# Input projection: 20 of 28 column blocks by seven quarter products, three selection tiles counted on ScalarE

## The chip, the cores and the metric

One core of one Trainium2 chip. The metric is the device time of one execution in microseconds (us), the median of several executions. TensorE is PE below, its weight loads PEld; VectorE is DVE, ScalarE is ACT, GpSimd is POOL, and SyncE (SP) only issues DMAs.

## The reference, cut to what matters

One inference step of a decoder trunk with two layers, all in float32. A prompt of 2048 tokens and 64 sample rows (8 sequences of 8 tokens) go through the same layers. Every layer starts with one combined input projection of the 1024 features of each token:

```python
h = jnp.einsum('btd,de->bte', x, w_in)
(cb, cc, ch, cg, sq, sk, sv, sg, dq, dk, dv, dg, iq, ik, iw) = split_in(h)
y_a = cb * conv(cc * ch) * silu(cg)              # 4 x 256 columns
y_b = stick_breaking(sq, sk, sv) * silu(sg)      # 4 x 384 columns
score = sum over 8 heads of relu(iq . ik) * iw   # the indexer
idx = top_k(score, 256)                          # per query
y_c = attend(rope(dq), rope(dk)[idx], dv[idx]) * silu(dg)
x = layer_norm(alpha * x + concat(y_a, y_b, y_c) @ w_out)
```

The keys and values, the last two rows of cc * ch and the new x are outputs too. The columns without the indexer's are 3584, which is 28 blocks of 128.

## The kernel before, in words

The program is written out by hand: each engine has one list of instructions per stage, with waits on semaphores, and a barrier of all engines stands between stages. A layer goes through seven of them: the indexer's projection and its scores for the prompt, the indexer for the samples (`sindex_*`), the input projection (`project_*` with `select_vector`), stick-breaking attention, sparse attention, the samples' attention, and the output projection. Memory is one tile, `arena`, that each stage cuts up anew; `banks` are the eight banks of PSUM, each 128 x 512 floats.

**PE in the projection** (`project_tensor`, lines 893 to 926). `xT` holds the tokens with the features on the partitions, in 8 chunks of 128 features. The 28 column blocks come in nine chunks of weights, `CHUNKS` (sk, c0, c1, dq, dkv, sv, sq, sg, dg); each is loaded while the one before it is used. Two kinds of units exist. A T unit (sk, dq, dkv, sv: 11 blocks) gives rows of 128 tokens: for each of 8 feature chunks a product with the tokens as weights and 384 or 256 columns moving (line 907). An F unit (c0, c1, sq, sg, dg: 17 blocks) gives 128 columns transposed: the weights stand and 512 tokens move (line 904). The 64 sample rows come once in each chunk (line 912). sk, dq and dk are needed in both forms, so their rows are transposed by PE as well (line 924, 112 transposes in a layer). A product in float32 is two instructions of PE in the profile; the counts in the profile are of those.

**ACT** (`project_scalar`) copies each unit out of its bank (lines 967, 969, 971), scales sq and dq, applies SiLU to the gates and copies the transposes (line 977). **POOL** (`project_gpsimd`) rotates dq and dk (the helper `rope`, lines 487 to 493) and computes the convolution with its gates (lines 1007 to 1024). **SP** (`project_sync`) stores everything and loads weights.

**DVE** (`select_vector`) takes no part in the projection: meanwhile it selects the 256 best scores of each query. The scores of 14 tiles of prompt queries (widths 384 to 2048) and of all sample queries (2056) lie in `arena`. In 32 passes it finds the threshold bit by bit: a pass counts for each tile how many scores reach the threshold (line 1057), writes the samples' comparison (line 1054), whose sum ACT takes (line 1044), and sets the next bit (lines 1073 and 1076). At the end, it marks the selected scores tile by tile, ties in order (lines 1082 to 1097). The next stage needs the marks, so the barrier waits for DVE too.

The output projection (lines 2281 on) already forms 2 x 2 blocks of its result from seven products in place of eight, with POOL and DVE making the sums. Its lines in the profile are used below.

## Time and profile before

| | us |
|---|---|
| median of 3 executions | 4497.47 |
| lowest, highest | 4490.78, 4499.33 |
| span of the profiled execution (first to last instruction) | 4494.1 |
| PE busy in it | 4186.5 (93%) |
| DVE busy | 3499.9 (78%) |
| ACT busy | 1748.9 (39%) |
| POOL busy | 1220.0 (27%) |

No time of the profiled execution other than its span is given; the span lies between the lowest and the highest of the three. The page divides the span into 40 slices and gives for each engine the busy share; shares over the whole span average stages with different limits, so the rows below are of single stages. A PE instruction's end is modelled, so durations of PE are best read as the distance between starts, or from the chain of waits.

### The profile page before, as it was taken

What the parts mean: (1) busy time and instruction counts of PE and PEld (TensorE: products, weight loads), DVE (VectorE), ACT (ScalarE), POOL (GpSimd) and SP (SyncE); (2) the same over time, 40 slices, a digit from 0 to 9 for tenths busy, and PEclk for the clock granted to TensorE, in tenths of its full rate; (3) what the DMA queues carried; (4) which work ended last, traced back from release to release, by engine and by line L of the source; (5) the groups of instructions that cost most, each with busy time, mean ns of one, the idle gap of its engine ahead of it and who ended that gap; (6) DMA issues with size and microseconds to landing.
All of it is one profiled execution on the core that took longest, in us unless ns stands there. A gap on an engine that the chain in (4) does not pass through costs nothing.

```text
span 4494.1 us, 81717 instructions
## 1 busy us (share of the span) xinstructions
PE 4186.5 (93%) x30510; PEld 2385.3 (53%) x30510; DVE 3499.9 (78%) x5677; ACT 1748.9 (39%) x2568; POOL 1220.0 (27%) x1531
## 2 busy tenths in 40 slices
PE   8988999999989999889989889999999999988898
PEld 5433545754466666454454335457544666764543
DVE  2686999999899865565637869999997998655656
ACT  3553211211067787340135632122111777873300
POOL 4220034500024242115442101355000333421154
PEclk9999999999999999889999999999999999998899
DMA  2102210211133102895311021112112330029942
...
DMA packets 328156, 397.11 MB, mean 88 GB/s; under 512 B 101079, under 2 KB 248626, under 8 KB 324434
## 3 DMA queue, kind: packets, MB, share of 16 engines
...
## 4 chain that ended last, share of the span: by engine, by line
PE 75%; DVE 7%; issue 6%; ACT 5%; DMA 4%; SPq 1%; ACTq 1%; POOL 1%; DVEq 0%; POOLq 0%
PE banks L904 21%; PE banks L907 14%; PE banks L2281 8%; PE banks L334 6%; PE banks L377 4%; PE banks L1549 3%; DVE arena L480 3%; PE banks L1519 3%; PE banks L1269 3%; PE banks L1231 2%; PE banks L1533 2%; PE banks L1253 2%; DVE arena L1376 1%; DMA arena<-in_cache_dsa_kv 1%; ACT arena L1579 1%
## 5 line engine op out<-in xcount | busy, mean ns | idle before, releaser
L1057 DVE TENSOR_SCALAR_CACHE_REDUCE arena<-arena 128x1920 uint8<-128x1920 f32 (+13 forms) x896 | 1259.0, 1474 | 0.0
L904 PE MATMUL banks<-arena 128*128 128x512 f32 x2176 | 937.4, 592 | 0.0
L904 PEld LDWEIGHTS banks<-arena 128*128 128x128 f32 x2176 | 410.6, 189 | 519.8 <-issue 519.5
L907 PE MATMUL banks<-arena 128*128 128x384 f32 (+1 forms) x2048 | 620.0, 459 | 2.4 <-POOLq L143 2.4
L1376 DVE TENSOR_TENSOR_SCAN arena<-arena 128x129 f32<-128x129 f32 (+3 forms) x480 | 512.3, 1127 | 22.1 <-ACT arena L1293 22.1
L480 DVE SCALAR_TENSOR_TENSOR arena<-arena 128x512 f32<-128x512 f32 (+3 forms) x532 | 404.4, 760 | 112.7 <-ACT arena L446 63.0
L907 PEld LDWEIGHTS banks<-arena 128*128 128x128 f32 x2048 | 380.8, 189 | 206.7 <-POOLq L143 2.6
L1614 DVE CUSTOM_DVE_ANT_0 arena<-banks,arena 128x512 f32<-128x512 f32 (+3 forms) x480 | 269.4, 607 | 159.5 <-PE banks L1519 158.8
L2281 PE MATMUL banks<-arena 128*128 128x512 f32 x896 | 387.2, 593 | 3.8 <-DVE arena L2407 1.7
L446 ACT ACTIVATE arena<-banks 128x1024 f32<-128x1024 f32 (+3 forms) x304 | 278.7, 920 | 236.6 <-PE banks L377 125.2
L377 PE MATMUL banks<-arena 64*128 64x512 f32 (+3 forms) x1216 | 309.5, 594 | 64.6 <-ACT arena L446 63.0
L334 PE MATMUL banks<-arena 128*128 128x292 f32 (+1 forms) x1088 | 312.9, 431 | 0.6 <-ACT arena L414 0.6
L971 ACT COPY arena<-banks 128x384 f32<-128x384 f32 (+2 forms) x144 | 70.5, 490 | 616.4 <-PE banks L907 361.3
L2281 PEld LDWEIGHTS banks<-arena 128*128 128x128 f32 x896 | 169.3, 190 | 218.9 <-issue 209.3
L1597 POOL TENSOR_SCALAR arena<-arena 128x128 f32<-128x128 f32 (+14 forms) x180 | 199.8, 1123 | 272.4 <-DVE arena L1625 272.4
L334 PEld LDWEIGHTS banks<-arena 128*128 128x128 f32 (+1 forms) x1088 | 191.7, 190 | 137.4 <-issue 89.4
L1307 ACT COPY arena<-banks 128x256 f32<-128x256 f32 (+3 forms) x240 | 216.1, 900 | 118.0 <-PE banks L1253 117.5
L1579 ACT COPY arena<-banks 128x1024 f32<-128x1024 f32 (+3 forms) x240 | 213.4, 889 | 121.1 <-PE banks L1533 120.4
L1567 ACT ACTIVATE arena<-arena 128x128 f32<-128x128 f32 (+15 forms) x192 | 231.1, 1204 | 4.0 <-DVE arena L1620 3.4
L1519 PE MATMUL banks<-arena 64*128 64x512 f32 (+3 forms) x960 | 211.2, 552 | 11.8 <-DVE arena L1614 9.8
L1549 PE MATMUL banks<-arena 128*64 128x128 f32 x3264 | 212.7, 277 | 8.3 <-DVE arena L1638 7.0
L1293 ACT ACTIVATE arena<-banks 128x256 f32<-128x256 f32 (+3 forms) x240 | 204.6, 896 | 36.0 <-PE banks L1231 21.7
...
## 6 DMA issues: line engine op xcount, KB each, us to landing
arena<-in_cache_sb_kv SPq DMA_DIRECT2D x256, 384.0 KB, 4.8
...
arena<-in_x_prompt SPq DMA_DIRECT2D x32, 512.0 KB, 3.9
...
arena<-xs SPq DMA_DIRECT2D x32, 512.0 KB, 4.0
arena<-in_cache_dsa_kv ACTq DMA_DIRECT2D x112, 128.0 KB, 5.3
...
```

Source lines behind the costliest of these rows:

```text
L334: m = nc.tensor.matmul(bank[v][r, 0:HALFW], xT[:, k, s * P:s * P + rows_of(s)], W1[:, k, v * HALFW:(v + 1) * HALFW], start=(k == 0), stop= ...
L377: k = nc.tensor.matmul(bank[4 + 2 * (i % 2) + e][:, 0:w], iqT[t % 2][a:a + HD, h, :], ikT[a:a + HD, c * FREE:c * FREE + w], start=True, st ...
L446: nc.scalar.activation(ir[b][:, :, 0:w], z[:, :, 0:w], ACT.Relu).then_inc(s_ir, 1)
L480: k = nc.vector.scalar_tensor_tensor(v, ir[b][:, h % 2, 0:w], wh, v, ALU.mult, ALU.add)
L904: m = nc.tensor.matmul(bank[i % 4][:, :], W2[c % 2][:, k, j * P:(j + 1) * P], xT[:, k, t * FREE:(t + 1) * FREE], start=(k == 0), stop=(k = ...
L907: m = nc.tensor.matmul(bank[i % 4][:, 0:WD[name]], xT[:, k, t * P:(t + 1) * P], W2[c % 2][:, k, 0:WD[name]], start=(k == 0), stop=(k == KC ...
L1057: nc.vector.tensor_scalar(dummy[j % 2][:, 0:v.shape[-1]], v, thr[:, t:t + 1], 0.0, ALU.is_ge, ALU.add, accum_out=history[:, k, t:t + 1]).t ...
L1376: nc.vector.tensor_tensor_scan(stay[n % 4][:, h, a:FREE + 1][:, ::-1], k, k, first, ALU.mult, ALU.min).then_inc(s_bs1, 1)
L1519: k = nc.tensor.matmul(bank[2 * (i % 2) + g][:, 0:w], dqT[q % 2][a:a + HD, c, t % 4 * P:(t % 4 + 1) * P], dkT[a:a + HD, x * FREE:x * FREE ...
L1549: k = nc.tensor.matmul(bank[6 + f % 2][a:a + HD, 0:P], dvn[:, kt, a:a + HD], weightsT(i)[:, o:o + P], start=(kt == 0), stop=(kt == t), ski ...
L1614: nc.vector.tensor_tensor_reduce(lg[e % 4][:, g, x * FREE:x * FREE + w], bank[2 * (i % 2) + g][:, 0:w], sc[:, SC_OFF[t] + x * FREE:SC_OFF[ ...
L2281: m = nc.tensor.matmul(bank[b], rows[:, k, :], cols[:, k, :], start=(first and k == 0), stop=(k == 3), skip_group_check=True)
```

## The change

**Products.** The 28 blocks are divided anew. 8 blocks (dq, dk; sv, dv) stay rows of 128 tokens, now in 34 units with 512 columns moving: first dq and dk ("qk"), then sv and dv ("vv"). The other 20 form ten pairs, `FBLOCKS`, and each pair is computed for two halves of 1024 tokens: 20 slots, m = 0 to 19. In a slot the result is 2 x 2 pieces (two blocks, two times 512 tokens), and the features are in two halves of 512. Seven products of 4 feature chunks each give what takes 8 such products in the old way. They stand in PE's list in the order 1, 6, 3 of the slot before, 5, 2, 7, 4; product 2 is added onto 1 in its bank, 7 onto 6, and 3 onto 5 after the bank has been read.

**Sums.** POOL makes, per half, four sums of tokens S1 to S4 (each 128 x 4 x 512) and, per slot, four sums of weights T1 to T4 (128 x 512 each). After the products, ACT copies banks to `fp1`, `fu2`, `fu3`; POOL adds `fp1` to `fu2` and `fu3` (`joined`); DVE adds a bank to one of them for three of the four pieces (`add_until`, 60 such adds in a layer, named "22", "21", "12" by token quarter and block). ACT applies SiLU to gated pieces in place. POOL does the convolution from the pieces in slots 1 to 4 and 11 to 14.

**Transposes and samples.** sk is now computed transposed and its rows come from PE's transposes; dq and dk as before: 112 transposes in a layer. The samples' rows come in 2 + 10 groups of 16 products, where nine were before.

**Selection.** From the second pass on DVE counts 11 tiles; the three longest (1792, 1920, 2048) are counted by ACT with `Sign(score - threshold)` and a sum, 93 counts in a layer. Their counts are compared with another bound (`cutv`). At the end DVE recounts these three twice to correct rounding. Where the adds stand among DVE's counts, and the counts among ACT's copies, is set by a table of due times in units of one product (4 chunks of 512 columns): `slot_at`, `unit_at`, `pass_at`, with PACE = 5.4 units for a pass.

**The rest.** `arena` grows by 4096 floats for each partition. Before the stage's barrier SP issues seven loads (six of 64 columns, one of 128) in place of one of 384. sq is no longer scaled when it is copied; the two sigmoids of the attention take the factor instead. Two buffers of the attention lie elsewhere. Weights of slot m + 1 are loaded after product 3 of slot m - 1.

```diff
--- before.py
+++ after.py
...
-            load_chunk(sp, l, 0)
...
+        PUNITS = [("qk", t) for t in ROWS_FIRST] + [("vv", t) for t in VALUES_FIRST]
...
+        FBLOCKS = (("cc0", "ch0"), ("cb0", "cg0"), ("cc1", "ch1"), ("cb1", "cg1"), ("sk0", "sk1"),
+                   ("sk2", "sq0"), ("sq1", "sq2"), ("sg0", "sg1"), ("sg2", "dg0"), ("dg1", "dg2"))
+        NFC = len(FBLOCKS)
+        NF2 = 2 * NFC
...
+        def load_row_weights(sp, l, v):
             src = w_in[l].rearrange("(c p) n -> p c n", p=P)
-            w, s = W2[c % 2], s_w2[c % 2]
-            if name in PERM:
+            if v == 0:
                 for h in range(HDSA):
                     d = (h % 3) * P + h // 3 * HD
-                    sp.dma_start(w[:, :, d:d + HD], src[:, :, COL[name] + h * HD:COL[name] + (h + 1) * HD]).then_inc(s, 16)
...
-                    a = col + P * (name == "c1")
-                    sp.dma_start(w[:, :, j * P:(j + 1) * P], src[:, :, a:a + P]).then_inc(s, 16)
+                    sp.dma_start(TW[0][:, :, d:d + HD], src[:, :, DQ + h * HD:DQ + (h + 1) * HD]).then_inc(s_tw[0], 16)
...
+        F_AT = 71.0
+        def slot_at(m, x):
+            extra = 0.7 * min(m, NFC - 1) + sum({5: 1.0, 6: 0.5}.get(e % NFC, 0) for e in range(m))
+            return F_AT + 7 * m + extra + x
...
+        def quarter(half, q, k):
+            a = (2 * half + q) * FREE
+            return xT[:, 4 * k:4 * k + 4, a:a + FREE]
...
+        def place(k, half):
+            if half:
+                return {"S3": quarter(0, 0, 0), "S2": quarter(0, 0, 1), "S4": quarter(0, 1, 1), "S1": quarter(1, 1, 0)}[k]
+            if k == "S1":
+                return quarter(0, 1, 0)
+            a = S_AT + (int(k[1]) - 2) * 4 * FREE
+            return arena[:, a:a + 4 * FREE].rearrange("p (c t) -> p c t", c=4)
...
+        def fbank(p, m):
+            return bank[{1: 4, 2: 4, 6: 5, 7: 5, 5: 6 + m % 2, 3: 6 + m % 2, 4: 0}[p]]
...
+            def onto_5(m):
+                fsummed(pe, l, m, "22")
+                fpool(pe, l, ("S4", m // NFC))
+                product(m, 3, wq(m, 1, 1), place("S4", m // NFC), first=False)
...
+            for m in range(NF2):
...
+                pe.wait_ge(s_w2[m % 2], at(s_w2[m % 2], 16 * (l * W2USES[m % 2] + loads)))
+                product(m, 1, wq(m, 0, 0), quarter(half, 0, 0))
+                if m:
+                    fevicted(pe, l, m - 1, "u3")
+                fpool(pe, l, ("S2", half))
+                fpool(pe, l, ("T2", m))
+                product(m, 6, fT[1], place("S2", half))
+                if m:
+                    onto_5(m - 1)
+                if m >= 2:
+                    fsummed(pe, l, m - 2, "12")
+                product(m, 5, fT[0], place("S1", half))
+                key_rows(m - 1, "11")
+                key_rows(m - 1, "22")
+                fevicted(pe, l, m, "p1")
+                product(m, 2, wq(m, 1, 0), quarter(half, 0, 1), first=False)
+                key_rows(m - 1, "21")
+                key_rows(m - 1, "12")
+                fevicted(pe, l, m, "u2")
+                fpool(pe, l, ("T3", m))
+                product(m, 7, wq(m, 0, 1), place("S3", half), first=False)
+                if m + 1 < NFC:
+                    sample(m + 1)
+                if m:
+                    fsummed(pe, l, m - 1, "21")
+                else:
+                    pe.wait_ge(s_pe, at(s_pe, l * NPE + NPU))
+                fpool(pe, l, ("T4", m))
+                product(m, 4, fT[2], quarter(half, 1, 1))
+            onto_5(NF2 - 1)
...
+                count_until(slot_at(m, 1))
+                fproduct(act, l, m, 1)
+                if m:
+                    fpool(act, l, ("u3", m - 1))
+                nc.scalar.copy(fp1, fbank(1, m)).then_inc(s_pe, 1)
+                count_until(slot_at(m, 2))
+                fproduct(act, l, m, 6)
+                if m:
+                    gate_piece(m - 1, "12", 10.3)
+                    fsummed(act, l, m - 1, "12")
+                nc.scalar.copy(fu2, fbank(6, m)).then_inc(s_pe, 1)
+                copy_key_rows(m - 1, "11")
+                copy_key_rows(m - 1, "22")
+                count_until(slot_at(m, 5))
+                fproduct(act, l, m, 2)
+                slot_free(act, l, m, "11")
...
+            def summed(name):
+                half = name[1]
+                a11, a12, a21 = quarter(half, 0, 0), quarter(half, 0, 1), quarter(half, 1, 0)
+                a22 = quarter(half, 1, 1)
+                out = place(name[0], half)
+                if name[0] == "S3":
+                    nc.gpsimd.tensor_tensor(out, a11, a21, ALU.subtract).then_inc(s_pp, 1)
+                elif name[0] == "S1":
+                    fpool(pool, l, ("S3", half))
+                    nc.gpsimd.tensor_tensor(out, a21, a22, ALU.add).then_inc(s_pp, 1)
+                elif name[0] == "S2":
+                    fpool(pool, l, ("S1", half))
+                    nc.gpsimd.tensor_tensor(out, place("S1", half), a11, ALU.subtract).then_inc(s_pp, 1)
...
+            def first_weight_sums(m):
...
+                if m:
+                    fproduct(pool, l, m - 1, 5)
+                nc.gpsimd.tensor_tensor(fT[0], wq(m, 0, 1), wq(m, 0, 0), ALU.subtract).then_inc(s_pp, 1)
...
+                nc.gpsimd.tensor_tensor(fT[1], wq(m, 1, 1), fT[0], ALU.subtract).then_inc(s_pp, 1)
...
+            def third_weight_sum(m):
...
+                nc.gpsimd.tensor_tensor(wq(m, 0, 1), wq(m, 1, 1), wq(m, 0, 1), ALU.subtract).then_inc(s_pp, 1)
...
+            def fourth_weight_sum(m):
...
+                nc.gpsimd.tensor_tensor(fT[2], wq(m, 1, 0), fT[1], ALU.subtract).then_inc(s_pp, 1)
...
+            def joined(m, name, out):
+                fevicted(pool, l, m, name)
+                nc.gpsimd.tensor_tensor(out, out, fp1, ALU.add).then_inc(s_pp, 1)
...
+        SIGNED = [NT - 1, NT - 2, NT - 3]
+        PASS = [NT, NT - 2, NT - 1] + [t for t in SELTILES if t < NT - 2]
+        PASS_V = [NT] + [t for t in SELTILES if t < NT - 3][::-1]
+        NCOUNT = len(PASS) + NBIT * len(PASS_V)
...
+        PACE, FIRST_PASS = 5.4, 7.4
...
+        def pass_at(k):
+            return 0.6 if k == 0 else FIRST_PASS + PACE * (k - 1)
...
+        def count_scalar(act, l, n):
+            k, j = scalar_count(n)
+            if j == 0:
+                act.wait_ge(s_cnt, at(s_cnt, counted_before(l, k) + 1))
+                nc.scalar.activation(compared[:, 0:NKEY], compared[:, 0:NKEY], ACT.Copy, accum_out=history[:, k, NT:NT + 1]).then_inc(s_sum, 1)
+            else:
+                t = SIGNED[j - 1]
+                v = scores(t)
+                act.wait_ge(s_bit, at(s_bit, l * NSTEP + 10 + 3 * (k - 1)))
+                act.wait_ge(s_sum, at(s_sum, l * NSUMS + n))
+                nc.scalar.activation(compared[:, 0:v.shape[-1]], v, ACT.Sign, bias=thr[:, t:t + 1],
+                                     accum_out=history[:, k, t:t + 1]).then_inc(s_sum, 1)
...
+            return {"22": slot_at(m, 6.9), "21": slot_at(m, 7.15), "12": slot_at(m + 1, 3.1)}[q]
...
+            def add_until(x):
+                while added[0] < NFSUM and vector_sum_at(added[0]) < x:
+                    m, q = FSUMS[added[0]]
+                    product, u, name = {"22": (5, fu3, "u3"), "21": (4, fu3, "u3"), "12": (3, fu2, "u2")}[q]
+                    slot_free(dve, l, m, q)
+                    fproduct(dve, l, m, product)
+                    fpool(dve, l, (name, m))
+                    nc.vector.tensor_tensor(hb[fslot(m, q)], fbank(product, m), u, ALU.add).then_inc(s_fsum, 1)
+                    added[0] += 1
...
-                for j, t in enumerate(PASS):
+                tiles = PASS_V if k else PASS
+                x, per = pass_at(k), PACE / sum(scores(t).shape[-1] for t in PASS_V)
+                for j, t in enumerate(tiles):
                     v = scores(t)
+                    add_until(x)
+                    x += per * v.shape[-1]
                     if t == NT:
-                        dve.wait_ge(s_sum, at(s_sum, l * NPASS + k))
+                        if k:
+                            dve.wait_ge(s_sum, at(s_sum, l * NSUMS + 1 + 4 * (k - 1)))
...
+                nc.vector.tensor_tensor(below, history[:, k + 1, :], cutv, ALU.is_lt).then_inc(s_bit, 1)
+                step(11 + 3 * k)
+                nc.vector.tensor_scalar(flip, below, float(1 << b), None, ALU.mult).then_inc(s_bit, 1)
...
+            x = pass_at(NPASS)
+            for j, t in enumerate(SIGNED):
+                v = scores(t)
+                add_until(x + 0.7 * j)
+                if j == 2:
+                    step(NTHR + 3)
+                nc.vector.tensor_scalar(dummy[j % 2][:, 0:v.shape[-1]], v, thr[:, t:t + 1], 0.0, ALU.is_gt, ALU.add,
+                                        accum_out=fix[:, t - NT + 3:t - NT + 4]).then_inc(s_bit, 1)
...
```

The lists of the three engines, as built:

PE, first layer. Before, the chunks sv and sq, behind the last transpose of the units before them (L907 rows of tokens, L904 blocks transposed, L912 samples; x16 are 8 feature chunks twice):

```order
L924 MATMUL banks<-ident,arena 128x128
L907 MATMUL banks<-arena 128x384 x120
L912 MATMUL banks<-arena 64x192 x16
L904 MATMUL banks<-arena 128x512 x96
L912 MATMUL banks<-arena 64x192 x16
```

The change, slots 4 and 5 (L1135 the quarter products, four to each; L1145 samples; L1155 transposes of sk):

```order
L1145 MATMUL banks<-arena 64x128 x16
L1135 MATMUL banks<-arena 128x512 x28
L1145 MATMUL banks<-arena 64x128 x16
L1135 MATMUL banks<-arena 128x512 x20
L1155 MATMUL banks<-ident,arena 128x128 x8
L1135 MATMUL banks<-arena 128x512 x4
L1155 MATMUL banks<-ident,arena 128x128 x8
L1135 MATMUL banks<-arena 128x512 x4
L1145 MATMUL banks<-arena 64x128 x16
```

A slot is 28 products of 512 columns where 32 stood for the same two blocks and 1024 tokens; samples come after every slot of the first half.

DVE, first layer. Before, the start of a pass (L1054 samples, L1057 counts):

```order
L1054 TENSOR_SCALAR arena<-arena 128x2056
L1057 TENSOR_SCALAR arena<-arena 128x1920
L1057 TENSOR_SCALAR arena<-arena 128x2048
L1057 TENSOR_SCALAR arena<-arena 128x384
L1057 TENSOR_SCALAR arena<-arena 128x512
L1057 TENSOR_SCALAR arena<-arena 128x640
```

The change, the start of a pass that runs beside the slots (L1509 samples, L1513 counts, L1496 the adds):

```order
L1509 TENSOR_SCALAR arena<-arena 128x2056
L1496 TENSOR_TENSOR arena<-banks,arena 128x512
L1513 TENSOR_SCALAR arena<-arena 128x1664
L1513 TENSOR_SCALAR arena<-arena 128x1536
L1513 TENSOR_SCALAR arena<-arena 128x1408
L1513 TENSOR_SCALAR arena<-arena 128x1280
L1513 TENSOR_SCALAR arena<-arena 128x1152
L1513 TENSOR_SCALAR arena<-arena 128x1024
L1496 TENSOR_TENSOR arena<-banks,arena 128x512
L1513 TENSOR_SCALAR arena<-arena 128x896
L1496 TENSOR_TENSOR arena<-banks,arena 128x512
```

The three longest counts are gone from the pass, and two or three adds that wait for PE and POOL stand between its counts.

POOL, first layer, the change, the middle of slot 11 (L1330, L1334 weights' sums T1 and T2; L1372 to L1384 a convolution; L1354 `joined`; L1340 T3). Before, no row of L1330, L1334, L1340 or L1354 existed:

```order
L1330 TENSOR_TENSOR arena<-arena 128x512
L1334 TENSOR_TENSOR arena<-arena 128x512
L1367 COPY arena<-arena 128x2
L1372 TENSOR_TENSOR arena<-arena 128x512
L1375 COPY arena<-arena 128x2
L1377 TENSOR_SCALAR arena<-arena 128x512
L1378 TENSOR_SCALAR arena<-arena 128x512
L1380 TENSOR_TENSOR arena<-arena 128x512
L1382 TENSOR_SCALAR arena<-arena 128x512
L1384 TENSOR_TENSOR arena<-arena 128x512
L1354 TENSOR_TENSOR arena<-arena 128x512
L1340 TENSOR_TENSOR arena<-arena 128x4x128
```

The sum `u3` (L1354) that DVE and then PE's product 3 need stands behind a whole convolution in such a slot.

## Rows read from the trace of the kernel before

**Rows 1.** The page: span, and part 1, busy time of each engine

```profile
span 4494.1 us, 81717 instructions
PE 4186.5 (93%) x30510; PEld 2385.3 (53%) x30510; DVE 3499.9 (78%) x5677; ACT 1748.9 (39%) x2568; POOL 1220.0 (27%) x1531
```

**Rows 2.** Busy time by stretch: the projection of both layers (columns: first row)

```profile
core 0: us, PE busy (x) PEld busy (x) DVE busy (x) ACT busy (x) POOL busy (x), PEclk, DMA share, GB/s
422.70:1232.80 810.10, 810.09 (x2512) 428.50 (x2512) 786.86 (x1057) 150.69 (x262) 162.38 (x280) 1.00 0.18 54
2655.30:3465.40 810.10, 810.08 (x2512) 428.47 (x2512) 786.87 (x1057) 150.62 (x262) 162.38 (x280) 1.00 0.18 54
```

**Rows 3.** Chain of waits, projection of layer 1: start, us, what

```profile
438.79 5.16 PE banks L907 x16
...
623.67 3.61 PE banks L912 x32
...
835.52 6.91 PE banks L907 x32
...
976.56 82.67 PE banks L904 x192
```

**Rows 4.** Timeline of PE: samples, and the stage's end

```profile
888.81 1.97 PE L912 MATMUL banks<-arena 128*64 128x128 f32 x32
...
1229.99 2.82 PE L912 MATMUL banks<-arena 128*64 128x192 f32 x32
1236.37 3.35 PE L1231 MATMUL banks<-arena 64*128 64x128 f32 x12 [3.56 <-SPq L143]
```

**Rows 5.** Timeline of DVE: two passes' starts, start and end of the marking

```profile
423.41 1.29 DVE L1054 TENSOR_SCALAR arena<-arena 128x2056 uint8<-128x2056 f32 x1
...
444.75 1.29 DVE L1054 TENSOR_SCALAR arena<-arena 128x2056 uint8<-128x2056 f32 x1
...
1110.69 0.72 DVE L1082 SCALAR_TENSOR_TENSOR arena<-arena 128x544 f32<-128x544 f32 x1
...
1214.18 2.36 DVE L1097 SCALAR_TENSOR_TENSOR arena<-arena 128x2056 f32<-128x2056 f32 x1
```

**Rows 6.** Groups by line and shape, 400 to 1260 us: busy, mean ns | idle before

```profile
L1057 DVE TENSOR_SCALAR_CACHE_REDUCE arena<-arena 128x2048 uint8<-128x2048 f32 x32 | 74.9, 2340 | 0.0
...
L1044 ACT ACTIVATE arena<-arena 128x2056 uint8<-128x2056 uint8 x32 | 61.4, 1919 | 0.0
...
L1054 DVE TENSOR_SCALAR arena<-arena 128x2056 uint8<-128x2056 f32 x32 | 41.9, 1310 | 1.4 <-DVE arena L1076 0.3
...
L1057 DVE TENSOR_SCALAR_CACHE_REDUCE arena<-arena 128x384 uint8<-128x384 f32 x32 | 19.4, 607 | 0.0
...
L969 ACT ACTIVATE arena<-banks 128x512 f32<-128x512 f32 x32 | 19.1, 597 | 189.7 <-PE banks L904 189.7
...
L1017 POOL TENSOR_SCALAR arena<-arena 128x512 f32<-128x512 f32 x16 | 12.2, 760 | 1.5
...
L1007 POOL TENSOR_TENSOR arena<-arena 128x512 f32<-128x512 f32 x8 | 10.2, 1276 | 109.8 <-ACT arena L969 109.7
...
L1093 DVE TENSOR_TENSOR_SCAN arena<-arena 128x2056 uint16<-128x2056 bf16 x1 | 4.4, 4442 | 0.0
```

**Rows 7.** Groups by line, output projection of layer 1, 2030 to 2260 us

```profile
L2281 PE MATMUL banks<-arena 128*128 128x512 f32 x448 | 193.5, 593 | 2.1 <-POOLq L143 1.5 <-DVE arena L2407 0.7
...
L2407 DVE SCALAR_TENSOR_TENSOR arena<-arena,banks 128x512 f32<-128x512 f32 x32 | 21.2, 682 | 38.6 <-PE banks L2281 38.6
...
L2209 POOL TENSOR_TENSOR arena<-arena 128x512 f32<-128x512 f32 x8 | 12.8, 1596 | 14.2 <-DMA arena<-mixT 11.8 <-PE banks L2281 2.4
...
L2197 POOL TENSOR_TENSOR arena<-arena 128x2048 f32<-128x2048 f32 x1 | 4.5, 4517 | 5.5 <-DMA arena<-in_w_out 5.5
```

**Rows 8.** DMA issues (KB each, us to landing), 400 to 1240 us

```profile
arena<-in_w_in SPq DMA_DIRECT2D x8, 512.0 KB, 6.1
...
arena<-in_w_in SPq DMA_DIRECT2D x12, 256.0 KB, 4.9
```

**Rows 9.** Timelines before the stage: SP's weight load, PE's last wait

```profile
401.03 0.44 SPq L813 DMA_DIRECT2D arena<-in_w_in  x1
...
408.73 1.97 PE L597 MATMUL banks<-ident,arena 128*128 128x128 f32 x8 [5.27 <-DMA arena<-in_cache_dsa_kidx]
```

874 lines of the change are left out of this document (581 added, 293 removed).

## The prediction

> **What bounds the kernel now.** I read the busy times first, then the table by stretch, the chain of waits in the stage, the timelines at its two ends, and the groups of its instructions. The span is 4494.1 us, PE busy for 93% of it [rows 1]; such a share tells little by itself, since stages differ. The table by stretch tells more: the projection is 810.1 us in either layer, 1620.2 us or 36% of the span, PE is busy for all of it at a granted clock of 1.00 (2.4 GHz), and DVE for 786.9 us [rows 2]. So two engines are full at once. Which of them ends the stage is read at its end: DVE's last mark begins at 1214.18 and is over at 1216.5 us [rows 5], PE's last samples begin at 1229.99, and the next stage begins at 1236.37 [rows 4]. PE bounds it, with DVE 16 us behind. Taking work from PE alone would therefore give 16 us in a layer at most; the reader should see why the change has to touch both.
>
> **PE, what goes.** An instruction of 512 columns costs 82.67 / 192 = 0.4306 us, of 384 columns 5.16 / 16 = 0.3225, of 256 columns 6.91 / 32 = 0.2159 [rows 3]. Before, a layer has 1088 of the first (17 blocks x 4 x 8 x 2), 768 of the second (9 blocks as 3 chunks x 16 x 8 x 2), 256 of the third: 468.5 + 247.7 + 55.3 = 771.5 us. After, 8 blocks as 2 x 16 units of 16 instructions are 512, and 20 slots of 7 products of 8 instructions are 1120, all with 512 columns: 1632 x 0.4306 = 702.7 us. That is **68.8 us less** in a layer. The transposes are 112 both times: nothing. Samples: before, six groups of 192 columns at 2.8 us, two of 256 at 3.6, one of 128 at 1.9 to 2.0 [rows 3, 4], 26.0 us; after, ten of 128 at 1.97 and two of 256, 26.9 us: **0.9 us more**. PE's own work goes from 810 to 742 us, 67.9 us less.
>
> Whether PE can run products of 4 chunks without pauses is seen in the output projection, which does so already: 448 instructions with 2.1 us of idle time before them [rows 7].
>
> **DVE, is it still covered?** A pass takes 444.75 - 423.41 = 21.34 us [rows 5]. A count costs 2340 ns at 2048 and 607 at 384 columns [rows 6], a slope of 1.04 ns, and less the overlap with its neighbour about 0.14 us + 1.04 ns a column. The three counts that leave have 5760 columns: 6.4 us less; one more small step of some 0.2 us: 15.1 us a pass. A layer: first pass 22, 31 passes 468, marking 1216.5 - 1110.7 = 106 [rows 5], recounts of 5760 columns twice 13 with steps 14, 60 adds of a bank at 0.68 (the output projection's [rows 7]) with gaps 43: 653 us against PE's 742. DVE is covered with 89 us to spare. Its adds wait in its list for PE and POOL, and behind a waiting add stand counts, behind those the next threshold, and ACT's counts wait for that; but as long as DVE is early, such a wait only keeps it in step.
>
> **ACT.** 2056 elements take 1919 ns [rows 6], so three counts of 5760 elements take 5.4 us and some tenths of a us each for start and reading the sum, 6.2, beside the 2.1 us for the samples' sum: 8.3 us of a pass of 18.6 us by the table. Copies at 0.6 us, four to seven in a slot of 24 to 26 us, add little. Covered; a copy can be late by one count, 2.2 us, against 6.9 us from product 7's end to product 6 of the next slot, which needs the copy.
>
> **POOL.** A sum of two tensors of 512 takes 1276 ns, a scaling 760 [rows 6], a sum of 2048 takes 4517 [rows 7]. A plain slot has six sums, 8 us of 24. S1 to S4 in slot 9 are 18 us more: 26 us, done before product 6 of slot 10 needs S2. In slots 1, 3, 11 and 13 two convolutions of 6.3 us stand in between. There the chain is: product 3 of the slot before ends 10.3 us into the slot, DVE adds (11.5), a convolution (18), u2, T1, T2 (22), the second convolution (28.6), u3 (29.9), DVE's add (30.7 and up to one count more). PE wants it for product 3, at 24.1 + 6.9 = 31.0 us in the second half, 33 in the first, where samples stand before it. So 0 to 2 us of waiting: I take 1 us x 4 = **4 us** a layer. Below it lies nothing; above, if all these sums took the 1596 ns of the output projection's [rows 7], the chain would be 3 us longer and the wait up to 4 us in each: 16 us.
>
> The Trainium skill (GPSIMD Engine Reference, Specifications) says that POOL's ports are shared with DVE and contended when DVE runs a two-port mode or reads two SBUF inputs. By this rule the chain keeps the 1276 ns, since DVE's counts and adds here read one SBUF tensor each; were the contention there all the same, it would be the 16 us.
>
> **DVE's marking.** The due times leave no room for adds there. Marking and recounts are 120 us, 5 slots; in these 15 adds of 0.7 us stand, 10.5 us of lag at its end. An add may be 6.5 us late before product 3 waits, less part of a scan of up to 4.4 us [rows 6] before it. I take **3 us**; bounds 0 and 10.5.
>
> **The stage's ends.** SP's one load of weights at 401.03 becomes seven; PE then waits 5.27 us for the last keys, which come while that load runs [rows 9]. A load of 256 KB lands in 4.9 us, of 512 KB in 6.1 [rows 8]. Queued in part before the keys, they delay the stage by **2 us** (bounds 0 and 6: one more load's time). All are in by 414, before the stage begins at 422.7. Within a slot, weights are asked for at 10.3 us and needed at 20.6 by the samples: 6.1 and an issue fit. At the end, product 3 is followed by an add, SiLU and a store, where samples' copies and a store made 3.56 us [rows 4]: **1.5 us** (0 to 4).
>
> **Sum.** In a layer -67.9 + 4 + 3 + 2 + 1.5 = -57.4 us, in both -114.8: 4494.1 becomes 4379.3 us. The median of the runs is 3.4 us above the profiled span, so I forecast **4382 us**. With all bounds at their ends a layer gives between 67.9 and 31.4 us: 4361 to 4434.
>
> **Rivals.**
> (a) *Nothing gives way*: every wait is covered, as in the output projection [rows 7]. The gain is 67.9 x 2: 4361 us. Against it: four engines in one chain in slots 1 and 3.
> (b) *The table's clock becomes the pace.* The due times let the last add stand at 223.4 units of 3.44 us, a stage of 769 us instead of 753: if static orders on DVE and ACT hold PE to it, the gain is 41 us in a layer, 4415 us. For it: three lists fixed by one table. Against it: PE's work sums to 215.5 units, no list waits for a clock, and DVE has 89 us.
> (c) *POOL is contended* as above: chains of 3 us more in the four heavy slots and slot 9, some 10 us a layer beyond mine: 4402 us.
> (d) *Slower than before.* The place is the chain from product 7 over ACT's copy, POOL's `joined`, DVE's add to product 3, in every slot. PE leaves it 10.3 us. The gain is 3.4 us a slot, so from a chain of 13.7 us on the change loses. I count 2.2 + 0.6 (ACT behind a count) + 1.3 + 2.6 (POOL behind two sums) + 1.9 + 0.7 (DVE behind a count) = 9.3 us with everything at its latest. If each queue held twice that, 18.6 us, PE would wait 8.3 us x 20 = 166 us in a layer against 67.9: 4497 + 2 x 98 = 4693 us.
> (e) *The change does not do what it says*: excluded in the order of instructions, where a slot has 28 products.
>
> **Chances.** Forecast's own case 0.45, (a) 0.18, (b) 0.16, (c) 0.13, (d) 0.06, something that leaves it within 0.2% (9 us, about what a measurement of this kernel can tell from no change) 0.02. The range takes (a) with the runs' spread and reaches up over (b) and (c): 4355 to 4422. Faster 0.92, same 0.02, slower 0.06.
>
> **What would show it.** Right: 1632 instructions of 512 columns per layer at 0.43 us; the stage 750 to 757 us in both layers; PE idle by 2 to 5 us in slots 1, 3, 11, 13 behind DVE's add or POOL, and little in plain slots; DVE busy for about 650 us; POOL's sums at 1.27 us. Wrong: PE idle in every slot of the first half behind DVE or ACT (b, d), POOL's sums at 1.6 us (c), PE waiting for weights, a granted clock below 1.00 in the stage, or stages after it that grow.

## The result, and the profile after

The changed kernel takes 4471.01 us (median of four runs, 4459.23 to 4475.12), the kernel before 4498.40 in the same comparison (4490.78 to 4499.99): a ratio of 0.9936, with a 95% interval of 0.9915 to 0.9958. It is faster by some 27 us, where 115 were forecast, and the time lies 49 us above the range. The profiled execution spans 4473.4 us against 4494.1 [rows 1].

The page of the changed kernel, span and part 1:

```profile
span 4473.4 us, 81130 instructions
PE 4084.7 (91%) x29742; PEld 2217.6 (50%) x29742; DVE 3328.3 (74%) x5531; ACT 2128.1 (48%) x2954; POOL 1620.4 (36%) x1591
```

Busy time by stretch, the projection of either layer from its first product to its last (columns: us, then busy time and instructions of each engine, the granted clock):

```profile
core 0: us, PE busy (x) PEld busy (x) DVE busy (x) ACT busy (x) POOL busy (x), PEclk, DMA share, GB/s
417.11:1217.16 800.05, 758.49 (x2128) 344.51 (x2128) 699.95 (x983) 340.12 (x456) 363.61 (x310) 0.98 0.23 67
2645.20:3445.64 800.44, 758.56 (x2128) 344.80 (x2128) 700.43 (x983) 340.14 (x456) 362.71 (x310) 0.98 0.23 67
```

Before, the stage took 810.1 us with PE busy for all of it [rows 2]. Now it takes 800.1, of which PE stands still for 41.6 us, and PE's own work is 758.5 us where I had counted 742. DVE is busy for 700 us, not 653.

By position in the span: the first layer's projection starts 5.6 us earlier than before, it and the store behind it take 9.6 us less, the stages between the two projections 5.0 us more, the second projection 9.2 us less, the rest 1.4 us less: 20.8 of the 20.7 us between the two profiled executions.

The same view of the first layer in three parts, before the slots, the first slots, the last:

```profile
420.00:650.00 230.00, 230.00 (x622) 105.73 (x622) 202.45 (x335) 120.11 (x162) 91.01 (x106) 1.00 0.17 54
650.00:900.00 250.00, 245.44 (x867) 116.60 (x864) 222.17 (x371) 137.09 (x182) 111.79 (x101) 0.99 0.26 72
900.00:1220.00 320.00, 280.16 (x636) 120.75 (x634) 273.35 (x272) 82.86 (x114) 160.81 (x104) 0.95 0.25 71
```

The first part is as forecast. The loss is in the third, which holds the last passes and the marking. PE's timeline there (start, busy us, in brackets the pause before it and what ended it):

```profile
1029.82 5.75 PE L1135 MATMUL banks<-arena 128*128 128x512 f32 x13
1041.14 26.75 PE L1135 MATMUL banks<-arena 128*128 128x512 f32 x56 [5.58 <-DVE arena L1496]
1074.97 9.72 PE L1135 MATMUL banks<-arena 128*128 128x512 f32 x16 [7.08 <-DVE arena L1496]
...
1121.90 17.02 PE L1135 MATMUL banks<-arena 128*128 128x512 f32 x32 [6.26 <-ACT arena L1274]
```

L1135 is a quarter product, L1496 DVE's add of a piece, L1274 ACT's copy of `fu2` or `fu3`. Behind the pause of 7.08 us sixteen instructions take 9.72 us, 0.61 each, where the kernel before had 0.4306 throughout [rows 3]. Such a pause is paid twice. Not every pause is: behind the one of 2.48 us before 778.26 eight instructions took 3.70 us at a granted clock of 1.00. Two stretches in the view by stretch: the first 5.4 us behind the pause of 7.08 us, at a mean granted clock of 0.52 (1.2 GHz for nearly all of it), and 30 us around the pause of 6.26 us:

```profile
1074.97:1080.40 5.43, 5.43 (x7) 2.35 (x8) 5.33 (x5) 0.00 (x0) 0.00 (x0) 0.52 0.25 97
1110.00:1140.00 30.00, 22.66 (x52) 9.70 (x50) 29.61 (x13) 3.23 (x6) 17.93 (x6) 0.83 0.22 68
```

**The two engines that lock each other out.** Timelines of DVE and of POOL at slot 9, while POOL makes the input sums S3 and S1:

```profile
898.43 4.32 DVE L1539 TENSOR_TENSOR arena<-arena 128x17 f32<-128x17 f32 x1
902.78 0.18 DVE L1541 TENSOR_SCALAR arena<-arena 128x17 int32<-128x17 f32 x1
902.99 4.37 DVE L1544 SCALAR_TENSOR_TENSOR arena<-arena 128x17 int32<-128x17 int32 x1
```

```profile
898.20 4.52 POOL L1314 TENSOR_TENSOR arena<-arena 128x2048 f32<-128x2048 f32 x1 [2.16 <-PE banks L1135]
902.79 4.54 POOL L1317 TENSOR_TENSOR arena<-arena 128x2048 f32<-128x2048 f32 x1
```

The two long DVE rows handle 17 columns and read two tensors in SBUF. Each ends about when POOL's sum ends. What the same step takes when nothing meets it is in the view of its line (least, median and longest ns of 31):

```profile
L1539 DVE TENSOR_TENSOR arena<-arena x31: 175/177/4318, 455.9 to 1024.9; 128x17 f32<-128x17 f32 x31
```

The lock works the other way too. DVE and POOL in the marking:

```profile
1132.50 4.83 DVE L1588 TENSOR_TENSOR_SCAN arena<-arena 128x1792 uint16<-128x1792 bf16 x1
1137.37 2.90 DVE L1591 SCALAR_TENSOR_TENSOR arena<-arena 128x1792 bf16<-128x1792 uint16 x1
```

```profile
1131.48 2.11 POOL L1354 TENSOR_TENSOR arena<-arena 128x512 f32<-128x512 f32 x1
1133.55 4.84 POOL L1340 TENSOR_TENSOR arena<-arena 128x512 f32<-128x512 f32 x1
1138.35 3.04 POOL L1346 TENSOR_TENSOR arena<-arena 128x512 f32<-128x512 f32 x1
```

POOL's sums of 512 columns, 1.276 us before [rows 6], take 4.84 and 3.04 us here. They alternate with DVE's operations, which are longer as well: the scan of 1792 columns took 3.89 us in the kernel before. The Trainium skill (SBUF — State Buffer, "Who interferes with whom") states just this: an exclusive lock for the whole instruction, taken by whichever of the two starts first, between a GpSimd instruction that reads SBUF and a DVE instruction with two SBUF inputs or in a two-port mode. By that rule the trace agrees, with 4.32 us for 17 columns, and it agrees too where it exempts the accumulating count: 355 counts in the stage have a mean of 1280 ns here and of 1281 ns in the run with narrow GpSimd sums.

How a pause then comes about, at 1121.90 us. The timelines of DVE, ACT and POOL:

```profile
1112.26 3.36 DVE L1588 TENSOR_TENSOR_SCAN arena<-arena 128x1536 uint16<-128x1536 bf16 x1
1115.65 1.82 DVE L1591 SCALAR_TENSOR_TENSOR arena<-arena 128x1536 bf16<-128x1536 uint16 x1
1117.51 1.82 DVE L1594 SCALAR_TENSOR_TENSOR arena<-arena 128x1536 f32<-128x1536 f32 x1
1119.36 1.09 DVE L1585 TENSOR_SCALAR arena<-arena 128x1664 bf16<-128x1664 f32 x1
1120.48 0.69 DVE L1496 TENSOR_TENSOR arena<-banks,arena 128x512 f32<-128x512 f32 x1
```

```profile
1121.26 0.59 ACT L1274 COPY arena<-banks 128x512 f32<-128x512 f32 x1 [20.22 <-DVE arena L1496]
```

```profile
1121.92 3.84 POOL L1354 TENSOR_TENSOR arena<-arena 128x512 f32<-128x512 f32 x1 [19.27 <-ACT arena L1274]
```

The add of piece "12" stands in DVE's list behind a tile's marking. ACT's copy of product 6 waits for that add, since `fu2` is one buffer and the add reads it; PE's next product waits for the copy; and POOL's join of `u2` waits for the copy and is then held for 3.84 us by DVE's next scan. The join feeds the sums and the join of `u3`, these the next adds. It is a closed circle through four engines, once round per slot.

### The profile page after: what moved, and what is told of

The parts are those of the page before. It is cut to its first block, busy times and chain, and to the rows that moved or that the text cites. A ratio compares the mean times of both kernels' runs of the same rounds, so it can differ in the third digit from the quotient of the medians.

```text
span 4473.4 us, 81130 instructions
## 1 busy us (share of the span) xinstructions
PE 4084.7 (91%) x29742; PEld 2217.6 (50%) x29742; DVE 3328.3 (74%) x5531; ACT 2128.1 (48%) x2954; POOL 1620.4 (36%) x1591
## 4 chain that ended last, share of the span: by engine, by line
PE 44%; DVE 15%; issue 7%; ACT 5%; POOL 2%; DMA 2%; SPq 2%; ACTq 0%; DVEq 0%; POOLq 0%
PE banks L2776 8%; PE banks L1135 5%; PE banks L1118 5%; PE banks L2048 3%; PE banks L335 3%; PE banks L2018 3%; PE banks L1768 3%; PE banks L1730 2%; PE banks L2032 2%; DVE arena L1513 2%; DVE arena L1588 2%; PE banks L1752 2%; PE banks L378 2%; DVE arena L1875 2%; DVE arena L481 1%
## 5 line engine op out<-in xcount | busy, mean ns | idle before, releaser
L1135 PE MATMUL banks<-arena 128*128 128x512 f32 x2240 | 1003.5, 607 | 83.4 <-DVE arena L1496 44.2
L1513 DVE TENSOR_SCALAR_CACHE_REDUCE arena<-arena 128x1664 uint8<-128x1664 f32 (+11 forms) x710 | 865.8, 1280 | 0.0
L1135 PEld LDWEIGHTS banks<-arena 128*128 128x128 f32 x2240 | 428.0, 193 | 634.6 <-issue 527.3
L1118 PE MATMUL banks<-arena 128*128 128x512 f32 x1024 | 445.0, 592 | 2.4 <-POOLq L144 2.4
L2776 PE MATMUL banks<-arena 128*128 128x512 f32 x896 | 387.3, 593 | 2.7 <-DVE arena L2902 1.3
L1476 ACT ACTIVATE arena<-arena 128x2048 uint8<-128x2048 f32 x186 | 352.9, 1897 | 7.9 <-ACT arena L1476 0.4
L1118 PEld LDWEIGHTS banks<-arena 128*128 128x128 f32 x1024 | 192.1, 190 | 232.2 <-issue 229.6
L2776 PEld LDWEIGHTS banks<-arena 128*128 128x128 f32 x896 | 168.9, 189 | 218.2 <-issue 210.2
L1354 POOL TENSOR_TENSOR arena<-arena 128x512 f32<-128x512 f32 x80 | 120.3, 1504 | 356.3 <-ACT arena L1274 296.9
L488 POOL TENSOR_TENSOR arena<-arena 128x288 f32<-128x288 f32 (+2 forms) x68 | 58.2, 856 | 489.2 <-ACT arena L415 378.9
```

Source lines behind the costliest of these rows:

```text
L1118: x = nc.tensor.matmul(bank[i % 4], xT[:, k, t * P:(t + 1) * P], TW[v][:, k, :], start=(k == 0), stop=(k == KC - 1))
L1135: x = nc.tensor.matmul(b, weights[:, k, :], rows[:, k, :], start=(first and k == 0), stop=(k == 3), skip_group_check=True)
L1476: nc.scalar.activation(compared[:, 0:v.shape[-1]], v, ACT.Sign, bias=thr[:, t:t + 1], accum_out=history[:, k, t:t + 1]).then_inc(s_sum, 1)
L1513: nc.vector.tensor_scalar(dummy[j % 2][:, 0:v.shape[-1]], v, thr[:, t:t + 1], 0.0, ALU.is_ge, ALU.add, accum_out=history[:, k, t:t + 1]).t ...
L2776: m = nc.tensor.matmul(bank[b], rows[:, k, :], cols[:, k, :], start=(first and k == 0), stop=(k == 3), skip_group_check=True)
```

## The experiments

Theory A: VectorE has no time left in the second half, because its instructions wait out GpSimd's and its marking takes longer; it is late with the adds. Theory B: the circle of add, copy, GpSimd sums and product is longer than a slot by itself. Theory C: the table of due times holds the lists back. Theory D came up after the first runs and was put to the test in the last three: the circle's length and VectorE's lateness add up. Ratios are to the kernel before, with 95% intervals. The kernel before had medians of 4498 to 4503 us in the five comparisons, so a difference of two times from different comparisons is uncertain by some 5 us. Stage times are of layer 1, like the 800.05 us above. Where a shortened sum, count or mark changes what is computed, the expectation says so; in x_split_s, e_table, e_order and the four kernels e_sign4 nothing is left out.

**1. VectorE's counts at 64 columns** (x_counts64)

```diff
-  nc.vector.tensor_scalar(dummy[j % 2][:, 0:v.shape[-1]], v, thr[:, t:t + 1], 0.0,
+  nc.vector.tensor_scalar(dummy[j % 2][:, 0:a], v[:, 0:a], thr[:, t:t + 1], 0.0 if k or t in SIGNED else 2048.0,
```

> VectorE's counts of passes 1 to 31 read 64 columns instead of the tile's width (pass 0 adds a constant so that thresholds stay finite): the thresholds, and so the mask, are not the reference's. GpSimd, ScalarE and TensorE issue what the changed kernel issues. Theory A (VectorE has no time left in the second half, because its instructions wait out GpSimd's and the recounts are late): the 37 us of TensorE pauses per layer and the lower clock behind them nearly vanish, a projection of 745 to 760 us instead of 804, the kernel at 4365 to 4390 us. Theory B (the circle of add, copy, GpSimd sums and product is itself longer than a slot, whatever VectorE does): the pauses stay, 4450 us or more. Theory C (the table of due times holds VectorE and ScalarE back): what waits is the order, so pauses stay at half or more, 4420 us or more.

Measured: 4418.35 us, ratio 0.9824 (0.9795 to 0.9854), stage 775.5 us. Of the 89 us missing against the forecast, 53 come back: PE still pauses eight times for over 1 us, all after 1015 us, beside the recounts and the marking. The time lies between A's 4390 and B's 4450, just under C's 4420, so this run alone decides nothing; A expected more.

**2. GpSimd's sums and joins at 64 columns** (x_pool_narrow)

```diff
-  nc.gpsimd.tensor_tensor(fT[1], wq(m, 1, 1), fT[0], ALU.subtract).then_inc(s_pp, 1)
+  nc.gpsimd.tensor_tensor(*cut(m, fT[1], wq(m, 1, 1), fT[0]), ALU.subtract).then_inc(s_pp, 1)
```

(`cut` keeps 64 columns from slot 1 on; the other sums of weights, the second half's input sums and all joins likewise. The first half's input sums and the convolutions stay whole.)

> GpSimd's sums of weights (slots 1 on), of the second half's inputs and its joins of u2 and u3 take 64 columns instead of 512 or 2048; the products 4 to 7 are then not the reference's. Convolutions, gates and rope stay. VectorE keeps all its work. Theory A: the compares, steps and marking that wait for GpSimd shrink (outside the convolution slots a compare 1.29 us, a mark 4.4 and 2.35 us), VectorE finishes its marking some 25 to 35 us earlier, projection 765 to 780 us, kernel at 4395 to 4425. Theory B (length of the circle): 4380 or less, since the circle loses some 8 us per slot. Theory C (table): 4450 or more, as VectorE's due times stay. So this run bounds contention and circle together; the run with narrow counts tells them apart.

Measured: 4382.28 us, ratio 0.9742 (0.9717 to 0.9767), stage 755.7 us, DVE busy 656.5 us. This is 13 us better than theory A allowed and within 3 us of the 4380 that theory B asked for. DVE got back 44 us, but the circle also got shorter, and this run does not part the two.

**3. The input sums in four pieces** (x_split_s)

```diff
+  for c in range(4):
+      k = nc.gpsimd.tensor_tensor(out[:, c, :], x[:, c, :], y[:, c, :], op)
+  k.then_inc(s_pp, 1)
```

> Each of GpSimd's eight input sums (128x2048, 4.54 us) is written as four of 128x512; only the last signals. Same result. Theory A: a VectorE compare or step that meets one waits at most about 1.3 us instead of 4.4 us; between 898 and 935 us of the first layer VectorE gains 8 to 10 us, GpSimd loses 2 to 3 us; kernel 5 to 12 us faster, 4460 to 4468. Theory B: nothing gained, up to 5 us slower, since the circle gets longer by the four starts. Theory C: no change.

Measured: 4458.23 us, ratio 0.9913 (0.9886 to 0.9939). DVE's timeline at the same place:

```profile
901.31 1.08 DVE L1545 TENSOR_TENSOR arena<-arena 128x17 f32<-128x17 f32 x1
902.42 1.19 DVE L1547 TENSOR_SCALAR arena<-arena 128x17 int32<-128x17 f32 x1
903.65 1.19 DVE L1550 SCALAR_TENSOR_TENSOR arena<-arena 128x17 int32<-128x17 int32 x1
```

Nothing on DVE was edited, and the step of 4.32 us takes 1.08; the step behind it, 0.18 us before, now meets a piece and takes 1.19. The longest wait went from POOL's 4.5 us instruction to the 1.2 us of a piece. That shows the lock and its length as a cause. In the kernel 13 us by the medians were gained where 5 to 12 had been expected; the intervals overlap, so this is not resolved.

**4. Another table** (e_table)

```diff
-        PACE, FIRST_PASS = 5.4, 7.4
+        EARLY, PACE, NEARLY, FIRST_PASS = 4.9, 5.3, 14, 7.1
```

> Only the table of due times: the first fourteen passes every 4.9 units from 7.1 on (now 5.4 from 7.4), the rest every 5.3, marking spread over 1.65 instead of 1.4 units per thousand columns. Same instructions on each engine, in another order on VectorE and ScalarE. Theory A: in the stretch before the quarter products VectorE's gap of 4 us in every second pass (it waits for ScalarE's late counts) goes, it is a pass further at slot 0 and ends 30 us earlier, so pauses shrink by half: projection 780 to 790 us, kernel at 4420 to 4445. Theory B: no change within 5 us. Theory C (table is the cause by itself): the whole 50 us per layer comes back, 4375 to 4400.

Measured: 4454.51 us, ratio 0.9900 (0.9875 to 0.9925), stage 790.7 us. Theory C as sole cause falls, since it wanted 4375 to 4400. DVE does more before the slots (223.3 us of 230 against 202.5), and some 16 us of the loss return, with intervals that just overlap. That is also less than theory A's 4420 to 4445: no range was met.

**5 and 6. The marking at 64 columns, alone and with the counts** (x_mark64, x_counts_mark64)

```diff
-                e, c = eqb[0:r, 0:v.shape[-1]], cum[0:r, 0:v.shape[-1]]
+                e, c = eqb[0:r, 0:64], cum[0:r, 0:64]
-                nc.vector.scalar_tensor_tensor(v, v, thr[0:r, t:t + 1], e, ALU.is_ge, ALU.subtract).then_inc(s_bit, 1)
+                nc.vector.tensor_scalar(v, v, thr[0:r, t:t + 1], None, ALU.is_ge).then_inc(s_bit, 1)
```

> The marking's equality test, running sum and tie rule take 64 columns; its last operation is a plain compare over the full width, so ties are marked otherwise than in the reference. All passes are whole. The marking of a layer falls from some 130 us to about 25. Theory A (VectorE late: half of it in the passes, half in the marking): the pauses before 1045 us of the first layer stay (about 17 us, and the clock), those behind it go: 785 to 790 us of projection, kernel 4445 to 4455. If the marking is the whole cause: 4410 or less. Theory B (length of GpSimd's circle): within 10 us of 4470.

> Both edits together, 64 columns in the counts of passes 1 to 31 and in the marking. VectorE keeps the compares, steps, adds and recounts; GpSimd and ScalarE keep everything. Counts alone gave 4418 us, with eight pauses left, all beside the marking. Theory A: at most 5 us of pauses per layer, projection 752 to 760, kernel 4375 to 4390. Theory B: pauses in the convolution slots remain, 4400 or more.

Measured: marking alone 4414.99 us, ratio 0.9815 (0.9798 to 0.9832), 30 us better than expected; both 4363.78 us, ratio 0.9695 (0.9676 to 0.9714). The gains against 4471 add up: 53 for the counts, 56 for the marking, 107 for both, and the last is 11 us more than the most that theory A had expected. The stage with both:

```profile
419.87:1163.33 743.46, 741.90 (x2128) 340.72 (x2128) 254.31 (x983) 341.50 (x456) 332.90 (x310) 1.00 0.25 72
```

PE's work is 741.90 us, my 742, with 1.6 us of pauses, and POOL does all its sums. So the circle by itself fits into a slot, also in the slots with convolutions: **theory B falls as a sole cause**. And the table in it is the changed kernel's: C falls again. POOL's rows from 1048 to 1182 us, first of the changed kernel (count, then least, median and longest ns), then of the kernel with a narrow marking:

```profile
L1354 POOL TENSOR_TENSOR arena<-arena x8: 1568/1975/3840, 1054.4 to 1165.0; 128x512 f32<-128x512 f32 x8
L1340 POOL TENSOR_TENSOR arena<-arena x4: 1583/2388/4843, 1065.3 to 1168.3; 128x512 f32<-128x512 f32 x4
```

```profile
L1354 POOL TENSOR_TENSOR arena<-arena x12: 1261/1266/2013, 1052.0 to 1181.4; 128x512 f32<-128x512 f32 x12
L1340 POOL TENSOR_TENSOR arena<-arena x5: 1263/1274/1277, 1060.0 to 1158.5; 128x512 f32<-128x512 f32 x5
```

Beside the marking a POOL sum takes one and a half times to twice its time in the median (1975 ns against 1266, 2388 against 1274), and two to three of them stand in the circle. That is why the marking costs more than its DVE time alone would: it delays adds and lengthens the circle at once.

**7 to 10. GpSimd light, VectorE's time given back** (x_narrow_pad, x_pad_all), **and the parts of GpSimd's work apart** (x_join_narrow, x_sums_narrow)

x_narrow_pad adds 42 us of counts in passes 1 to 31 to x_pool_narrow:

```diff
+                    if k and t in (2, 3):
+                        v = scores(8)[:, 0:1100]
```

x_pad_all widens three of the marking's four operations as well:

```diff
+                more = w if t >= NT - 1 else min(SEQ, w + 620)
+                e, c = eqb[0:r, 0:more], cum[0:r, 0:more]
```

> The kernel with narrow GpSimd sums (4382 us), and VectorE given back the 44 us per layer that the shorter waits for GpSimd had saved it: in passes 1 to 31 the counts of tiles 2 and 3 read 1100 columns of tile 8 in place of their own 384 and 512, 1.36 us more per pass by the rows, 42 us per layer. GpSimd stays out of the way. Products 4 to 7 and the masks of tiles 2 and 3 are not the reference's. Theory A (what GpSimd's sums cost is VectorE's time, not the length of the circle): most of the gain goes again, 4440 to 4465 us. Theory B (the shorter circle was the gain): 4382 to 4400. Halfway (4420) would mean that both count.

> The last kernel with narrow GpSimd sums and padded counts (4403 us), with the marking's first three operations widened by up to 620 columns too, 27 us per layer by the rows (3.94 ns a column). VectorE then works about as long as in the changed kernel, 690 to 700 us per layer, beside a GpSimd that is short. Masks and products 4 to 7 are not the reference's. Theory A (only VectorE's time counts): back to 4455 to 4475. Theory D (the circle's length and VectorE's lateness add up, and a pause comes when the sum passes the slot of 24 us): between, 4420 to 4445. If the marking's length costs nothing with a short circle: 4400 to 4410.

> The changed kernel, with only the joins of u2 and u3 on GpSimd cut to 64 columns (products that use them are not the reference's): 2.4 us less in the circle of each slot, GpSimd meets VectorE in two of six sums less. VectorE keeps its work. Theory D: the pauses shrink by about 2 us in each slot that has one, 10 to 15 us per layer with the clock, kernel 4440 to 4455. Theory A: 4460 or more (contention falls by a few us only).

> The opposite: joins whole, the sums of weights from slot 1 on and the second half's input sums cut to 64 columns. T1 and T2 stand between the two joins (2.5 us of the circle), T3 and T4 behind them; contention falls by most of its 44 us. Theory A: most of the 89 us of the run with all sums narrow, 4385 to 4400. Theory D: about two thirds of it, 4400 to 4420; and the gains of the two runs together give the 89 us, more or less.

(Of x_pad_all only the time and the lengths of DVE's rows are used.)

| kernel | us | ratio (95%) | stage, us | DVE busy | POOL busy |
|---|---|---|---|---|---|
| changed | 4471.0 | 0.9915 to 0.9958 | 800.1 | 700.0 | 363.6 |
| x_pool_narrow | 4382.3 | 0.9717 to 0.9767 | 755.7 | 656.5 | 235.4 |
| x_narrow_pad | 4403.5 | 0.9757 to 0.9795 | 762.0 | 697.4 | 235.4 |
| x_pad_all | 4449.8 | 0.9877 to 0.9910 | | | |
| x_sums_narrow | 4404.0 | 0.9766 to 0.9806 | 764.1 | 664.7 | 275.0 |
| x_join_narrow | 4430.6 | 0.9830 to 0.9863 | 780.4 | 683.4 | 322.4 |

In x_narrow_pad DVE is busy for 697 us as in the changed kernel, beside a short POOL, and the stage is 38 us shorter; theory A wanted 4440 to 4465, and 4403.5 lies just above theory B's 4382 to 4400. But this padding lies in the passes alone, and part of what DVE had got back lay in the marking. With the marking made longer as well, the time is 4449.8, between theory D's 4420 to 4445 and theory A's 4455 to 4475, so the ranges alone do not decide. The work does: the marking's rows are 129.4 us here and 104.3 in x_narrow_pad, so DVE works some 722 us, 22 more than in the changed kernel, and the kernel is still 21 us faster, with intervals apart. This is where **theory A in its plain form falls**: some 21 us or more are the shorter circle's. Of the 89 us of x_pool_narrow, 21 went with 42 us of counts and 46 with 25 us of marking a layer: time in the marking is the dearer. The joins alone give 40 us, 9 more than theory D expected at most, the other sums 67, together more than the 89 of both, so they relieve the same pauses. What stands is theory D: the circle's length and the adds' lateness add up. That a pause comes just where their sum passes the slot of 24.1 us fits these runs, but none measured it. The lock feeds both.

**11. The join of u3 ahead of the second convolution** (e_order)

```diff
-                if c in (1, 3):
-                    convolve(m - 1, "2")
                 joined(m, "u3", fu3)
+                if c in (1, 3):
+                    convolve(m - 1, "2")
```

> GpSimd joins u3 before it convolves the second token block, not after, in the four slots with a convolution. Theory A: VectorE's adds stand less long behind the join in those slots (two of the pauses, 2.5 us and 2.1 us at 721 and 778 us, and one near 920 go), VectorE is some 10 us less late: kernel 4450 to 4465. Theory B (the circle's length decides): much more, 4430 or less, since the circle is 7 us shorter in four slots. If the later end of the convolution delays an add that needs its buffer: no change or up to 10 us slower.

Measured: 4458.67 us, ratio 0.9909 (0.9892 to 0.9925). The first pause of the slots, 2.07 us at 721.53, goes and the second stays at 2.64 us; the profiled stage is 798.4 us. The time is as near to the changed kernel's as theory A said: where the join stands against the convolution is not the main cost. On top of four tiles by signs it gave nothing either (4413 against 4404 us, intervals overlapping).

**12 to 15. A tile more on ScalarE** (e_sign4, _b, _c, _d)

```diff
-        SIGNED = [NT - 1, NT - 2, NT - 3]
+        SIGNED = [NT - 1, NT - 2, NT - 3, NT - 4]
-        PACE, FIRST_PASS = 5.4, 7.4
+        EARLY, PACE, NEARLY, FIRST_PASS = 4.5, 5.1, 14, 7.1
-                x += 1.4e-3 * w + 0.2
+                x += 2.5e-3 * w + 0.2
```

(shown for e_sign4_b; all four have the input sums in pieces and the step numbers that go with a fourth tile.)

> Same result as the reference with ScalarE counting four tiles by signs, VectorE ten of them and the compare (1.87 us less in each of 31 passes, 58 us per layer, plus 3.6 us for two more recounts); the input sums in four pieces, the join of u3 ahead of the second convolution, and a new table (first fourteen passes every 4.5 units, the rest every 5.1, marking over 2.0 units per thousand columns). Theory A: VectorE has 60 us of room per layer again, pauses fall below 10 us: projection 755 to 770, kernel 4375 to 4405. Theory B: no better than the reordered kernel alone. Against it: ScalarE needs 10 us of each pass and evicts products too; if its counts come late, 4420 or more.

> The kernel with four tiles counted by signs (4430 us), with the convolution back ahead of the join of u3, and the marking spread over 2.5 instead of 2.0 units per thousand columns, so that its table time (about 165 us) is no shorter than its work with the adds in it (144 us). The pauses left at 998 to 1142 us of the first layer lay beside the marking, behind an add that stood after a 3 to 6 us row of marking instructions. Theory A with the table's marking too tight: those pauses shrink, 4405 to 4420. If the order of the join was what helped before: 4430 to 4440.

> As the last, but with the join of u3 ahead of the second convolution. VectorE was seen to wait 5 to 7 us for the end of that convolution, whose buffer its add needs. If that wait matters: slower than the run without it by 5 us or more; if the join ahead is a gain, 5 to 10 us faster than it. Marking's table as in the last: below 4430 either way.

> As the run with the convolution first, later passes every 4.85 units instead of 5.1 and the marking over 2.7: more of the passes ahead of their time, more room for the marking. The passes need 17.1 us each beside the adds by the sum of rows, 4.85 units are 16.6 us: VectorE would be a little late in each pass and less late in the marking. Within 5 us of it if the two balance, 10 us or more slower if passes then hold up the adds.

| kernel | passes / marking in the table | convolution 2 | us | ratio (95%) | stage, us |
|---|---|---|---|---|---|
| e_sign4 | 5.1 / 2.0 | behind the join | 4430.4 | 0.9831 to 0.9864 | 778.2 |
| e_sign4_b | 5.1 / 2.5 | ahead | 4404.4 | 0.9764 to 0.9798 | 764.5 |
| e_sign4_c | 5.1 / 2.5 | behind the join | 4413.1 | 0.9789 to 0.9826 | 766.6 |
| e_sign4_d | 4.85 / 2.7 | ahead | 4434.8 | 0.9823 to 0.9866 | 778.1 |

The first of them missed its range of 4375 to 4405 by 25 us; the others show that much of this was its table. e_sign4_b computes what the reference does, and **beats both kernels**: 99 us or 2.2% below the kernel before in the same comparison. Its stage, and DVE's waits in it:

```profile
422.82:1187.28 764.46, 747.72 (x2128) 341.36 (x2128) 631.95 (x926) 394.76 (x518) 377.53 (x334) 0.99 0.24 70
```

```profile
L1502 DVE TENSOR_TENSOR arena<-banks,arena 128x512 f32<-128x512 f32 x59 | 39.9, 688 | 101.4 <-POOL arena L1360 84.6 <-PE banks L1135 15.8 <-issue 0.7
```

L1502 is the add there, L1360 the join. The adds now wait 101 us, 63 in the changed kernel over the same stage: DVE is early. After 1042 us PE has no pause left; the six of over 1 us that remain, 16 us in all, lie before, most of them in slots with convolutions. A wider marking in the table was worth 17 us (e_sign4 against _c, from two comparisons), 0.25 units off each later pass, spent on the marking, cost 30 (_d against _b): with static lists, where the table puts the adds matters as much as the work it orders.

## Why the prediction was wrong

**PE's own work** was right: 1632 instructions of 512 columns at 0.4306 us and samples make 742 us, and where nothing stops PE the trace has 741.90. Rival (a)'s 4361 us is the time of the kernel in which DVE is light, 4363.78. The 89 us above the forecast come from pauses and from the clock behind them.

**"DVE is covered with 89 us to spare"** is the step that failed. The terms were taken from a kernel in which POOL was busy for 162 of 810 us [rows 2]. In the changed kernel it is busy for 364, and in passes and marking the compare, the small steps and the marking's operations wait for it at times. Groups of DVE in the stage (busy us, mean ns):

```profile
L1588 DVE TENSOR_TENSOR_SCAN arena<-arena 128x384 uint16<-128x384 bf16 (+14 forms) x15 | 47.5, 3164 | 0.4
L1509 DVE TENSOR_SCALAR arena<-arena 128x2056 uint8<-128x2056 f32 x31 | 47.2, 1522 | 1.1
...
L1539 DVE TENSOR_TENSOR arena<-arena 128x17 f32<-128x17 f32 x31 | 14.8, 476 | 28.5 <-ACT arena L1476 27.8
L1544 DVE SCALAR_TENSOR_TENSOR arena<-arena 128x17 int32<-128x17 int32 x30 | 14.5, 484 | 1.0
```

The compare takes 1522 ns instead of 1310 [rows 6], 7 us a layer; the small steps take 476 and 484 ns in the mean where the median is 177, and with a third such step (L1541, 335 ns) that is 23 us; the marking's four operations take 123.1 us against 104.3 in x_pool_narrow, 19 us. Together that is about the 700 - 653 = 47 us; with POOL's sums narrow, 44 of them go (656.5). Worse, the spare time was counted over the stage and is needed in its last third, where beside the marking DVE is busy for 29.6 of 30 us (1110 to 1140).

**The contention rule was applied to the wrong instructions.** I wrote that the chain keeps POOL's 1276 ns, because DVE's counts and adds read one SBUF tensor each. That is true of them, and the counts kept their time. But compare, steps, scan, both tie rules and the equality tests of the marking, some 210 us of the stage, are not counts or adds, and I looked only at what the contention does to POOL. It acts on both. Rival (c) priced it at 10 us a layer through chains of 1596 ns; the sums in the marking took 1975 to 2650 ns in the median, up to 5383.

**The chain of rival (d) was cut one link short.** I followed product 7, copy, join, add, product 3. The add of "12" behind product 3 holds ACT's copy of product 6, as `fu2` is a single buffer, and the copy the joins of the next slot. So lateness is not absorbed at product 3 but handed on. My "+4" for convolution slots and "+3" for marking were sized on the open chain. Measured: 41.6 us of pauses, where those two terms make 7: 34.6 us too few.

**The clock after a pause** was not priced at all: PE's work is 758.5 us instead of 741.9, so 16.6 us a layer. The two make 51.2 us a layer, which is the stage's 800.1 against the 742 + 7 of my terms.

**The ends.** The start was forecast 2 us later and came 5.6 us earlier. One execution does not settle that term: in the runs above, whose program is the same up to there, the stage starts between 414.8 us (x_mark64) and 424.0 us (e_sign4). The store at the stage's end was forecast at +1.5 us on 3.56 [rows 4] and is 4.05. The 5.0 us by which the stages between the projections grew are not explained; no run looked into them. In span, two layers of 51.2 us too few, -7.6 for the start, +3.0 for the stages between, -2.0 for the two ends and -1.4 for the rest make up the 94 us between the 4379.3 of the sum and the 4473.4 measured.

**Rival (b)**, the table as the pace at 4415 us, gave a time nearer the truth by a mechanism that is not there by itself: with the same table and a light DVE the stage takes 743.5 us.
